# Two pairs of gate/up groups of each feed-forward part computed with seven block products in place of eight

## The reference

```python
def swiglu(x, wg, wu, wd):
    return (jax.nn.silu(x @ wg) * (x @ wu)) @ wd        # 1024 -> 2816 -> 1024

for l in range(DEPTH):                                   # second block
    x = x + 0.5 * swiglu(rmsnorm(x, ffn1_norm[l]), ffn1_wg[l], ffn1_wu[l], ffn1_wd[l])
    ...                                                  # three attention mixers, w_out
    x = x + 0.5 * swiglu(rmsnorm(x, ffn2_norm[l]), ffn2_wg[l], ffn2_wu[l], ffn2_wd[l])
```

## Time and profile before

| | |
|---|---|
| median of three runs | 1607.0 us (1606.98 to 1607.59) |
| span of the profiled execution | 1606.2 us; the page shows no other time of it |
| busy, share of the span | TensorE 99%, VectorE 66%, ScalarE 55%, GpSimd 6% |
| DMA | 270 MB, 168 GB/s over the span |
| granted TensorE clock | 1.00 |

### The profile page before, as it was taken

The page is one execution under the profiler, slowest core; times in us unless marked ns, Lnnn a source line. Parts: engine busy times, 40 slices in busy tenths (PEclk is TensorE's granted clock), DMA queues, the critical chain, the costliest instruction groups (busy, mean ns, idle before and its releaser), DMA issues.

```text
span 1606.2 us, 23049 instructions
## 1 busy us (share of the span) xinstructions
PE 1585.8 (99%) x8924; PEld 1337.3 (83%) x8924; DVE 1061.8 (66%) x1312; ACT 882.2 (55%) x1322; POOL 93.2 (6%) x184
## 2 busy tenths in 40 slices
PE   9999999999999999999999999999999999999998
PEld 8778888877888888888877888888888887788887
DVE  6867566786766676656758566667666666766665
ACT  7755444675544555444657554445544556654444
POOL 1000000030000020000030000002000003000000
PEclk9999999999999999999999999999999999999999
DMA  8326655523555558565530465557655452065552
GB/s 293 124 79 210 209 180 187 184 89 134 193 190 193 183 180 255 183 200 181 167 132 2 132 209 183 189 180 223 220 177 190 157 182 80 7 204 196 180 190 89
DMA packets 187607, 270.45 MB, mean 168 GB/s; under 512 B 4968, under 2 KB 147552, under 8 KB 187536
## 3 DMA queue, kind: packets, MB, share of 16 engines
q1 hardware_dynamic: 184560, 261.87, 48.9%
q0 software_dynamic: 2544, 7.09, 1.7%
q10 hardware_dynamic: 432, 0.53, 0.1%
HBM read 268.42 MB, written 1.05 MB: 168 GB/s over the span
## 4 chain that ended last, share of the span: by engine, by line
PE 93%; DVE 3%; ACT 2%; issue 1%; DMA 0%; POOL 0%; POOLq 0%; SPq 0%; DVEq 0%; ACTq 0%
PE pair L2268 29%; PE pair L2272 15%; PE bank L2144 8%; PE bank L2145 8%; PE bank L2146 8%; PE bank L2238 6%; PE bank L2211 3%; PE pair L2485 2%; PE bank L2536 1%; PE bank L2506 1%; PE pair L2144 1%; PE pair L2146 1%; PE pair L2145 1%; PE pair L2092 1%; PE pair L2310 1%; PE bank L2429 1%
## 5 line engine op out<-in xcount | busy, mean ns | idle before, releaser
L1346 DVE TENSOR_TENSOR w_lo<-raw,w_hi 128x2048 fp32r<-128x2048 f32 (+2 forms) x239 | 543.7, 2280 | 132.2 <-ACT w_hi L872 131.2
L872 ACT ACTIVATE w_hi<-raw 128x2048 fp32r<-128x2048 f32 (+2 forms) x243 | 461.7, 1905 | 262.1 <-PE pair L2272 191.6
L2268 PE MATMUL pair<-xt,w_hi 128*128 128x512 f32 x2064 | 494.1, 391 | 0.1
L2268 PEld LDWEIGHTS pair<-xt,w_hi 128*128 128x128 f32 x2064 | 382.6, 188 | 76.7 <-issue 0.5
L2272 PEld LDWEIGHTS pair<-xt,w_lo 128*128 128x128 f32 x2064 | 265.8, 191 | 10.8
L2272 PE MATMUL pair<-xt,w_lo 128*128 128x256 f32 x2064 | 269.1, 283 | 0.0
L2144 PE MATMUL bank<-w_hi,hid_hi 128*128 128x512 f32 x528 | 206.5, 391 | 0.0
L2145 PE MATMUL bank<-w_hi,hid_lo 128*128 128x512 f32 x528 | 206.2, 390 | 0.0
L2146 PE MATMUL bank<-w_lo,hid_hi 128*128 128x512 f32 x528 | 205.4, 389 | 0.0
L1431 DVE TENSOR_TENSOR gate_sum<-pair,gate_sum 128x512 f32<-128x512 f32 x66 | 45.6, 691 | 200.1 <-ACT gate_sum L1008 200.1
L2146 PEld LDWEIGHTS bank<-w_lo,hid_hi 128*128 128x128 f32 x528 | 99.2, 188 | 21.1
(11 more groups left out here) (316 smaller groups left out, 1740.4 us busy)
## 6 DMA issues: line engine op xcount, KB each, us to landing
raw<-in_w_gate_up SPq DMA_DIRECT2D x44, 1024.0 KB, 5.1
raw<-in_ffn_wg SPq DMA_DIRECT2D x44, 1024.0 KB, 5.3
raw<-in_ffn_wu SPq DMA_DIRECT2D x44, 1024.0 KB, 5.3
raw<-in_ffn_wd SPq DMA_DIRECT2D x44, 1024.0 KB, 5.0
raw<-in_w_down SPq DMA_DIRECT2D x22, 1024.0 KB, 4.9
raw<-in_w_in SPq DMA_DIRECT2D x21, 1024.0 KB, 5.2
raw<-in_w_o SPq DMA_DIRECT2D x8, 1024.0 KB, 5.2
raw<-in_w_out SPq DMA_DIRECT2D x8, 1024.0 KB, 5.0
```

Of the source, the lines that this page charges most:

```text
L872: act.activation(w_hi[s][:, 0:filled(u)], raw[s][:, 0:filled(u)], ACT.Copy).then_inc(hi_ready, 1)
L1346: dve.tensor_tensor(w_lo[s][:, 0:filled(u)], raw[s][:, 0:filled(u)], w_hi[s][:, 0:filled(u)].bitcast(F32), ALU.subtract)\
L2268: pe.matmul(out[:, 512 * m:512 * (m + 1)], w[0][:, c, P * m:P * (m + 1)], xt[:, 2 * SEQ * c:2 * SEQ * (c + 1)], start=(c == 0), stop=False)
```

## The change

In every part groups 4 and 5, and groups 8 and 9, are computed together. For such a pair the 256 tokens and the 1024 features of the activations are each cut in two, giving four blocks. The weights are the 512 gate columns and the 512 up columns of the pair, cut into upper and lower features, which gives four quarters of 512 x 512 (1 MB each): gate upper (`LEFT`), up upper (`UPPER`), gate lower (`LOWER`), up lower (`RIGHT`). Seven products (a variant of Strassen's scheme) take the place of eight. Each uses one block of the activations or a sum of them as stationary and a quarter, or a sum of quarters, as moving operand: 12 matmuls of 512 columns (`product`). Each product's weights are a unit that is rounded and split like the others, so a part has 39 units (`FU`) and not 33.

The four quarters get tiles of their own (`fold_raw`), filled by `load_set` outside the ring of three. VectorE makes the four sums of quarters in place (`make`), and once a part the four sums of the activation blocks (`whole_rows`, `row_sums`, `row_sums_rest`). The results come out with tokens as rows. ScalarE copies them out of the banks where they must be added up again, VectorE adds them, and the hidden tiles are turned by eight transposes on TensorE at the end of the pair. Between the products stand the down units of the two groups before. The products use banks 0 to 3, the same as the gate and up results, so the first waits for the group before to be summed up (`gate_summed`), and the third for its up result (`up_summed`). The hardware loop is gone on all engines: the groups are written out one by one.

```diff
--- before.py
+++ after.py
@@ -33,6 +33,20 @@
...
+FOLD_GROUPS = (4, 8)
+FOLD_FIRST = (10, 25)
+PLAIN_GROUPS = (0, 1, 2, 3, 6, 7, 10)
+PLAIN = {g: i for i, g in enumerate(PLAIN_GROUPS)}
+NP = len(PLAIN_GROUPS)
+LEFT, UPPER, LOWER, RIGHT = range(4)
+FOLD_TILE = {0: LEFT, 1: LOWER, 4: LEFT, 5: RIGHT, 6: UPPER, 7: LOWER}
+FOLD_SUM = {2: 1, 6: 2, 4: 3, 7: 4}
...
@@ -300,13 +314,20 @@
...
+        xs_lo = [sb(f"xs_lo{i}", UW, F32R, at=(o_base, m_base)[i]) for i in range(2)]
+        xs_sum = [sb(f"xs_sum{i}", UW, at=(o_base, m_base)[i]) for i in range(2)]
         memt = sb("memt", 2 * KC * SEQ, F32R)
         mem_end = room[0]
-        qk_table = sb("qk_table", 8 * HD, at=f_base + 17 * 1024)
...
@@ -599,9 +652,17 @@
...
+        GATE_AT = {0: 0, 1: 2, 2: 5, 3: 8, 6: 20, 7: 23, 10: 35}
+        UP_AT = {0: 1, 1: 3, 2: 6, 3: 9, 6: 19, 7: 24, 10: 34}
+        DOWN_AT = {0: 4, 1: 7, 2: 13, 3: 18, 4: 21, 5: 22, 6: 28, 7: 33, 8: 36, 9: 37, 10: 38}
+        SLOT_FREED = {6: 4, 7: 5, 10: 8}
...
@@ -642,14 +703,31 @@
...
+            def load_fold(tile, src):
+                sp.dma_start(fold_raw[tile][:, :].rearrange("p (c n) -> p c n", c=4), src)\
+                  .then_inc(fold_landed[tile], 16)
+            def load_set(u0, k, wg, wu):
+                if k == 0:
+                    sp.wait_ge(unit_used, u0)
+                else:
+                    sp.wait_ge(lo_ready, u0 + FOLD_FIRST[k - 1] + 8)
+                first = 256 * FOLD_GROUPS[k]
+                load_fold(LEFT, quarter(wg, 0, first))
+                load_fold(UPPER, quarter(wu, 0, first))
+                load_fold(LOWER, quarter(wg, 1, first))
+                load_fold(RIGHT, quarter(wu, 1, first))
             u = OPENING
...
@@ -659,22 +737,44 @@
...
+                load_gate(2)
+                load_up(2)
+                load_set(u, 0, wg, wu)
+                load_down(1)
+                load_gate(3)
+                load_up(3)
+                load_down(2)
+                load_down(3)
+                load_up(6)
+                load_gate(6)
+                load_set(u, 1, wg, wu)
+                load_down(4)
+                load_down(5)
...
@@ -1001,45 +1105,141 @@
...
+                def split_quarter(k, place):
+                    u = u0 + FOLD_FIRST[k] + place
+                    act.wait_ge(fold_landed[FOLD_TILE[place]], 16 * (fold_index(f, k) + 1))
+                    rounded(u)
+                def split_sum(k, place):
+                    act.wait_ge(fold_made, 4 * fold_index(f, k) + FOLD_SUM[place])
+                    rounded(u0 + FOLD_FIRST[k] + place)
+                def product_copied(k, place, to, src):
+                    act.wait_ge(unit_used, u0 + FOLD_FIRST[k] + place + 1)
+                    act.activation(to[:, :], src, ACT.Copy).then_inc(fold_copied, 1)
...
+                def fold_hidden(k):
+                    act.wait_ge(fold_turned, fold_index(f, k) + 1)
+                    for b in range(2):
+                        act.activation(hid_hi[b][:, :], bank[b], ACT.Copy).then_inc(hidden_hi, 1)
+                def fold(k, gates, up, hidden):
+                    v = u0 + FOLD_FIRST[k]
+                    split_quarter(k, 0)
+                    split_quarter(k, 1)
+                    gates()
+                    split_sum(k, 2)
+                    up()
+                    product_copied(k, 0, gate_sum[0], bank[0])
+                    split_hi(v + 3)
+                    split_sum(k, 4)
+                    hidden()
+                    product_copied(k, 2, gate_sum[1], bank[2])
+                    split_quarter(k, 5)
+                    fold_act(k, 0)
+                    split_sum(k, 6)
+                    product_copied(k, 4, up_sum[0], bank[0])
+                    split_sum(k, 7)
+                    split_hi(v + 8)
+                    product_copied(k, 6, gate_sum[0], bank[0])
+                    split_hi(v + 9)
...
@@ -1424,34 +1624,173 @@
...
+                def whole_rows():
+                    dve.wait_ge(turned_lo.sem, turned_lo.n)
+                    both_ = xt[:, :].rearrange("p (c v s) -> p c v s", c=KC, v=2).bitcast(F32)
+                    dve.tensor_tensor(whole, both_[:, :, 0, :], both_[:, :, 1, :], ALU.add).then_inc(xs_order, 1)
+                def row_sums():
+                    a11, a12 = (whole[:, 4 * r:4 * r + 4, 0:P] for r in range(2))
+                    a21, a22 = (whole[:, 4 * r:4 * r + 4, P:SEQ] for r in range(2))
+                    dve.wait_ge(xs_order, 5 * f + 1)
+                    dve.tensor_tensor(sums[:, 0], a22, a21, ALU.subtract).then_inc(xs_order, 1)
+                    dve.tensor_tensor(sums[:, 2], a11, a21, ALU.subtract).then_inc(xs_order, 1)
+                    dve.wait_ge(xs_order, 5 * f + 2)
+                    dve.scalar_tensor_tensor(sums[:, 1], sums[:, 0], -1.0, a11, ALU.mult, ALU.subtract)\
+                       .then_inc(xs_order, 1)
+                    dve.wait_ge(xs_order, 5 * f + 4)
+                    dve.scalar_tensor_tensor(sums[:, 3], sums[:, 1], -1.0, a12, ALU.mult, ALU.subtract)\
+                       .then_inc(xs_order, 1)
...
+                def row_sums_rest():
+                    dve.wait_ge(xs_rounded, f + 1)
+                    dve.tensor_tensor(xs_lo[f >= 2][:, :], xs_sum[f >= 2][:, :], xs_hi[:, :].bitcast(F32),
+                                      ALU.subtract).then_inc(xs_ready, 1)
...
+                def make(out, a_, b_):
+                    dve.tensor_tensor(out[:, :], a_[:, :], b_[:, :], ALU.add).then_inc(fold_made, 1)
+                def upper_sum(k):
+                    landed(k, LEFT, UPPER)
+                    dve.wait_ge(lo_ready, split_before[u0 + FOLD_FIRST[k] + 2] + 1)
+                    make(raw_of(u0 + FOLD_FIRST[k] + 2), fold_raw[LEFT], fold_raw[UPPER])
+                def right_sum(k):
+                    landed(k, RIGHT)
+                    dve.wait_ge(fold_made, 4 * fold_index(f, k) + 1)
+                    make(fold_raw[UPPER], fold_raw[UPPER], fold_raw[RIGHT])
+                def three_sum(k):
+                    dve.wait_ge(fold_made, 4 * fold_index(f, k) + 1)
+                    dve.wait_ge(lo_ready, u0 + FOLD_FIRST[k] + 1)
+                    make(fold_raw[LEFT], raw_of(u0 + FOLD_FIRST[k] + 2), fold_raw[RIGHT])
...
+                def four_sum(k):
+                    landed(k, LOWER)
+                    dve.wait_ge(fold_made, 4 * fold_index(f, k) + 3)
+                    dve.wait_ge(lo_ready, u0 + FOLD_FIRST[k] + 2)
+                    make(fold_raw[LOWER], fold_raw[LEFT], fold_raw[LOWER])
...
+                def fold(k, g):
+                    v = u0 + FOLD_FIRST[k]
+                    split_lo(v)
+                    gates(g)
+                    three_sum(k)
+                    split_lo(v + 1)
+                    four_sum(k)
+                    split_lo(v + 2)
+                    add_up(g)
+                    multiply(g)
+                    split_lo(v + 3)
+                    first_gate(k)
+                    hidden_rest(g)
+                    split_lo(v + 4)
+                    split_lo(v + 5)
+                    split_lo(v + 6)
+                    first_up(k)
+                    fold_multiply(k, 0)
+                    split_lo(v + 7)
+                    split_lo(v + 8)
+                    second_up(k)
+                    second_gate(k)
+                    split_lo(v + 9)
+                    fold_multiply(k, 1)
+                    split_lo(v + 10)
+                    fold_rest(k)
...
@@ -2319,17 +2676,78 @@
...
+                def product(u, out, x_, more=False):
                     s = u % RING
-                    pe.wait_ge(lo_ready, u + 1 + 6 * i)
-                    pe.wait_ge(hidden_lo, base + g + 1)
+                    hi, lo = x_
+                    pe.wait_ge(hi_ready, u + 1)
+                    for c in range(4):
+                        w = w_hi[s][:, 512 * c:512 * (c + 1)]
+                        pe.matmul(out, hi[c], w, start=not more and c == 0, stop=False,
+                                  skip_group_check=more)
+                        pe.matmul(out, lo[c], w, start=False, stop=False, skip_group_check=more)
+                    pe.wait_ge(lo_ready, u + 1)
+                    for c in range(4):
+                        end = pe.matmul(out, hi[c], w_lo[s][:, 512 * c:512 * (c + 1)], start=False,
+                                        stop=(c == 3), skip_group_check=more)
+                    end.then_inc(unit_used, 1)
+                def fold_products(k, g, downs):
+                    v, n = u0 + FOLD_FIRST[k], fold_index(f, k)
+                    pe.wait_ge(gate_summed, base + PLAIN[g] + 1)
+                    product(v, bank[0], x_part(0, 0))
+                    product(v + 1, bank[1], x_part(0, 1))
+                    pe.wait_ge(up_summed, base + PLAIN[g] + 1)
+                    pe.wait_ge(xs_ready, f + 1)
+                    product(v + 2, bank[2], sum_part(0))
+                    down(downs[0])
```

(39 more changed lines are left out.)

393 lines of the change are left out of this document (281 added, 112 removed).

## The result

| | before | after |
|---|---|---|
| median of the runs, us | 1606.99 (1606.98 to 1607.59) | 1688.77 (1686.27 to 1692.86) |
| span of the profiled execution, us | 1606.2 | 1684.5 |
| mean granted TensorE clock | 1.000 | 0.981 |

The change makes the kernel slower: ratio 1.0511, 95% interval 1.0497 to 1.0526. The forecast was 1642 us with a range of 1612 to 1668. The direction is right, the time lies 21 us above the range, and 47 above the forecast. On the span the change costs 78.3 us where the sum had 35.3.

The account below looks back on a forecast made before the run. TensorE, busy 99% of the span, was taken as the bound. Saving 26.5 us, adding 8.5 us of waits in six parts and 5.4 in two, gave +35.3 on 1606.2: forecast 1642 us, range 1612 to 1668.

Parts of the forecast that it names:

- TensorE's saving: Seven products and eight transposes replace four projection units: 2.2 us less TensorE work a pair, 26.5 us over twelve pairs.
- First pair, 4.2: At the third product TensorE waits 4.2 us for VectorE's up sum of group 3, in every part.
- Second pair, 2.4: TensorE waits 2.4 us for VectorE's up sum of group 7, in every part.
- Third and fifth part, 5.4 each: Late loads, beside GpSimd's table loads, delay the first pair's up sum: 9.0 us instead of 3.5, 5.4 more each.
- Down unit 4 and small waits, 11.4: Per part, 0.9 us at down unit 4 behind the quarters' loads and 1.0 us at down units inside the pairs.
- The clock: Rival: new waits drop TensorE to 1.2 GHz, up to 8 us each time, mostly 1650 to 1690 us; chance 10%.
- The granted clock should stay at 1.00: Sign to check in the profile after: no fall of TensorE's clock from the 2.4 GHz level.
- the six long ones: The waits of 4 us and, in two parts, 9, after which the clock rival let the clock fall.
- 1691: The clock rival's upper time in us: the forecast 1642 plus 49 for low clock after six long waits.
- The work is hidden: Rival: VectorE runs ahead in its idle third, TensorE keeps its 2.2 us a pair, 1580 us; chance 10%.
- Half hidden: Rival: VectorE's queue is 2 to 3 us a pair shorter, the pair breaks even, 1595 to 1615 us; chance 7%.
- The 28 us of queue against 27.6 of TensorE work: First pair, gate unit 2 to the third product: VectorE's queue against TensorE's work, cited against the work being hidden.

Follow-up runs that it names:

- e2: The changed kernel with the four sums of quarters covering only 128 of 2048 columns: 1617.78 us, 1.0063 of before.
- e6: The changed kernel with the VectorE order of e5 and the load order of e4 together: 1603.08 us, 0.9977 of before.
- e4: The changed kernel with only the load order changed, down units 1 and 4 ahead of the quarters, last two quarters later: 1665.17 us, 1.0370 of before.
- e1: The changed kernel with TensorE's long waits filled by matmuls that add zero: 1673.36 us, 1.0412 of before.
- e5: The changed kernel with VectorE's movable work ordered by when TensorE needs each result, loads unchanged: 1636.21 us, 1.0187 of before.
- e7: The changed kernel with the fourth sum of quarters moved from ahead of the up sum to behind the fifth product's split: 1645.17 us, 1.0241 of before.
- e3: The changed kernel with the four sums of quarters made by GpSimd in place of VectorE: 1775.21 us, 1.1055 of before.

## Why the forecast was wrong, point by point

**TensorE's saving.** Right. Products take 2.72 to 2.77 us, 2.74 in the mean (e2), for 2.73. A pair's eight transposes take 0.79, and the first matmul behind them 0.08 more than its usual 0.23, together the 0.88 of the sum. e2's timeline of the transposes:

```profile
200.54 1.03 PE L2738 MATMUL pair<-cst,hid 128*128 128x128 f32 x8
201.33 0.94 PE L2625 MATMUL pair<-xt,w_hi 128*128 128x512 f32 x3
```

e6's busy time, corrected for the clock, is some 20 us under before's against 26.5; most of the rest is the cost around each wait that is described under "Not named".

**First pair, 4.2.** Measured 4.01 to 4.03 in all six parts, through the steps named: queue 28.4 (28.3), start at 151.33 (151.25), landing at 145.30 (145.4).

**Second pair, 2.4.** Measured 2.60, 3.36 in one part. Right.

**Third and fifth part, 5.4 each.** Measured 6.36 and 4.60, from the loads (in the third, ScalarE waited 10.61 us for the DMA, and e4 takes the waits away). The size is right. The place is not: the forecast had one wait of some 9 at the up sum, and the trace has one at down unit 1 and one behind it, at the up sum, that stays 4.0.

**Down unit 4 and small waits, 11.4.** Found 17.4: down unit 4 waits up to 1.67 and not 0.9 (6.5 in all parts against 5.4), the down unit behind the seventh product 0.43 to 0.48 and the second product 0.30, together 7.3 against the 6.0 of the small waits, and a wait of 0.34 to 0.86 for the gate sum ahead of the first product was not in the list.

**The clock.** This is the step that failed: the sum put the clock at nothing, and the trace has 26 us of it, the largest of the terms that make up the 43 us between 35.3 and 78.3 (the others are 9.9 not named, 6.0 in small waits and 1.1 in the large ones). The sum's own check was "The granted clock should stay at 1.00", and it stood as a rival at 10%, priced for "the six long ones". Three things were off. First, its place: it is no other course of events but the consequence of waits that the sum itself forecast at 73%, twelve of 2.4 us and more, where the longest in the trace of before was 1.1. With no row for a wait of 4 us, a cost between 0 and the rival's own price for a wait should have stood in the sum, with both ends. Second, its reach: it followed the first up sum in all six parts and four of the second's 2.6 us waits. Third, its price a time: 3.41 or 6.83 us at the low level, so 1.6 us (the third product, 4.37 against 2.77) to 3.4, not the 8.2 I let it have. Twelve stretches make 26 us; of the 21 that e1 gives back, 12 to 15 show in the time. The two errors in the rival partly cancel, which is how its 1691 comes near 1688.77; that is no credit to its working. The page I named for it (the Trainium skill, TensorE: Matmul & The Clock Gate, HAM oscillation) warned that idle gaps between bursts of matmuls send TensorE to the low clock; the trace agrees, with the granted clock of 0.50 and the 0.43 us spacing behind ten of the twelve up sum waits and both late down units.

**Not named, 9.9.** The view of waits counts idle time only. Around a wait the last matmul stands as 0.39 us busy where its successor would have come after 0.228, and the first takes 0.34 before the next starts (250.90 to 251.24): 0.27 us a wait. So 0.16 us of each wait is booked as work, and the 4.01 us at the first up sum are 4.17 of delay for the 4.2 forecast. 43 waits make 11.6 us, e6's 17 make 4.6, where 6.9 are unnamed (-4.3 of span + 26.5 - 12.3 - 3). The sizes fit; no experiment took this cost alone, so it is argued and not shown.

**The rivals on the fast side.** "The work is hidden" and "Half hidden" are false for this order. e6 shows that they failed by the order of two queues and not by the amount of work. The 28 us of queue against 27.6 of TensorE work, which I held against them, took the order as given.

## What to carry to other kernels

Where an added operation makes TensorE wait longer than any wait in the trace of before, put the clock into the sum with both ends, and count the places from your own list of waits. A queue's average (here 75% of VectorE) says nothing of whether work is hidden: count what stands in front of each result that the bound engine needs, and move what does not belong there before judging the change; here two reorderings without a new instruction were worth 86 us and turned the sign. Test two causes together as well as singly: e5 alone took 52.6 us off and e4 alone 23.6, each stayed above before, and both together took 85.7, which is 9.5 more than the two added.

## What the runs showed of the hardware

In after, TensorE's clock fell to 1.2 GHz at waits of 4.0 us six times in six and of 2.6 us four times in five, while one of 3.36 us had no such effect; in e7 it fell at waits of 1.6 us three times in six. The low stretches of after were 3.41 or 6.83 us long, and some in e2, e3 and e5, at waits of 6 us and more, 10.24, with matmuls of 512 columns 0.43 us apart instead of 0.228. Filling the waits at the up sums with matmuls that add zero kept the clock there, and the product came only 0.08 us later (16 of 0.228 in a wait of 4.0, 179.84 for 179.76). A GpSimd addition of two 128x2048 fp32 tiles took 4.62 us, and a VectorE operation with two tiles as inputs, issued meanwhile, stood until it ended (0.69 us became 4.68, 2.28 became 6.58); one with a bank as an input did not (0.69). Eight fp32 transposes of 128x128 took 0.79 us, in e2 and in after alike.
